# Attention scores of two mixers with high and low parts stacked to 128 rows

## The reference

```
# fox_branch, for each block of 128 queries
logits = (einsum('bhtd,bhsd->bhts', qb, kb) * scale + F[:, :, q0:q1, None] - F[:, :, None, :q1])
probs  = softmax(where(mask, logits, -inf));  outs.append(einsum('bhts,bhsd->bhtd', probs, vb))
# mixer_b, for each grid row
s = einsum('bnqhd,brnjhd->bhnqrj', q_r, k_reg) * scale + bias     # neighbourhood keys
s_ctx = einsum('bnqhd,bchd->bhnqc', q_r, kc) * scale              # context keys
p = softmax(concatenate([s, s_ctx]));  o = p_lat @ v_reg + p_ctx @ vc
```

## Time and profile before

| what | us |
|---|---|
| median of 3 runs | 3241.89 (3241.35 to 3244.12) |
| span of the profiled execution | 3236.3 |
| PE busy | 3109.7, 96% |
| DVE busy | 1999.7, 62% |
| ACT busy | 1299.9, 40% |
| POOL busy | 759.8, 23% |
| a turn of `fox` (first score to first score) | 77.0 |
| a turn of `nb` | 95.5 |

### The profile page before, as it was taken

How to read it: one execution, slowest core, us unless ns; L and a number is a source line. 1 busy time by engine, 2 the same in 40 slices (tenths; PEclk the granted TensorE clock), 3 DMA queues, 4 the chain that set the end, 5 groups by cost and what they waited for, 6 DMA issues and landing times.

```text
span 3236.3 us, 47842 instructions
## 1 busy us (share of the span) xinstructions
PE 3109.7 (96%) x18134; PEld 2578.9 (80%) x18134; DVE 1999.7 (62%) x3834; ACT 1299.9 (40%) x2340; POOL 759.8 (23%) x324
## 2 busy tenths in 40 slices
PE   9999999999999989999899999999899999999987
PEld 6888888777777767877799889888677778777765
DVE  5676677555565657975755555556755555655555
ACT  5534443444444440022444444440344444454412
POOL 3223332322222213543211121113112112111221
PEclk9999999999999999999999999999999999999999
DMA  3111111111111137521200010153201111100141
GB/s 118 46 40 46 46 59 46 60 59 53 53 53 53 64 146 298 220 79 52 91 30 30 31 43 30 46 203 130 78 21 51 45 51 45 51 32 33 67 161 76
DMA packets 64828, 237.79 MB, mean 73 GB/s; under 512 B 7008, under 2 KB 10080, under 8 KB 63600
## 3 DMA queue, kind: packets, MB, share of 16 engines
q1 hardware_dynamic: 31680, 115.91, 9.9%
q10 hardware_dynamic: 32944, 119.10, 9.7%
HBM read 185.11 MB, written 49.87 MB: 73 GB/s over the span
## 4 chain that ended last, share of the span: by engine, by line
PE 79%; DVE 9%; ACT 5%; issue 2%; DVEq 2%; DMA 1%; ACTq 1%; SPq 0%
PE ps L1304 21%; PE ps L189 13%; PE ps L360 9%; PE ps L2223 7%; PE ps L1368 5%; PE ps L1334 4%; PE ps L1350 4%; PE ps L891 3%; PE ps L482 3%; PE ps L868 2%; PE ps L133 2%; DVE fox_l L1455 1%; PE ps L852 1%; DVE wa_l L941 1%; PE ps L853 1%
## 5 line engine op out<-in xcount | busy, mean ns | idle before, releaser
L210 POOL TENSOR_TENSOR w_hi<-raw,small 128x1024 fp32r<-128x1024 f32 x160 | 334.9, 2093 | 2393.7 <-PE ps L1304 1099.3
L212 POOL TENSOR_TENSOR w_lo<-raw,w_hi 128x1024 fp32r<-128x1024 f32 x160 | 424.8, 2655 | 22.8
L1304 PE MATMUL ps<-nb_u_hi,w_hi 128*128 128x512 f32 (+1 forms) x640 | 249.2, 389 | 6.1 <-DVE nb_q_lo L2470 4.2
L1304 PE MATMUL ps<-nb_u_hi,w_lo 128*128 128x512 f32 (+1 forms) x640 | 246.6, 385 | 0.0
L1304 PE MATMUL ps<-nb_u_lo,w_hi 128*128 128x512 f32 (+1 forms) x640 | 245.7, 384 | 0.0
L1466 DVE TENSOR_TENSOR nb_pt_lo<-ps,nb_pt_hi 128x512 fp32r<-128x512 f32 x208 | 143.9, 692 | 144.2 <-ACT nb_pt_hi L1393 143.9
L360 PE MATMUL ps<-u_hi,w_hi 128*128 128x512 f32 x528 | 212.8, 403 | 5.9 <-ACT silu_h L539 2.6
L1304 PE MATMUL ps<-u_hi,w_lo 128*128 128x512 f32 x512 | 208.9, 408 | 0.0
L360 PE MATMUL ps<-u_hi,w_lo 128*128 128x512 f32 x528 | 208.6, 395 | 0.0
L360 PE MATMUL ps<-u_lo,w_hi 128*128 128x512 f32 x528 | 208.4, 395 | 0.0
L1304 PE MATMUL ps<-u_hi,w_hi 128*128 128x512 f32 x512 | 208.3, 407 | 0.0
(11 more groups left out here) (357 smaller groups left out, 8027.8 us busy)
## 6 DMA issues: line engine op xcount, KB each, us to landing
raw<-in_w_stream SPq DMA_DIRECT2D x160, 512.0 KB, 3.3
h_sb<-in_w_ada ACTq DMA_DIRECT2D x16, 1024.0 KB, 5.0
nf_b<-nf_rows ACTq DMA_DIRECT2D x16, 512.0 KB, 4.4
nb_bias<-in_rel_bias ACTq DMA_DIRECT2D x16, 448.0 KB, 3.8
y_parts<-wa_y_hi ACTq DMA_DIRECT2D x8, 640.0 KB, 3.0
y_parts<-wa_y_lo ACTq DMA_DIRECT2D x8, 640.0 KB, 4.2
la_out_yh<-y_parts SPq DMA_DIRECT2D x8, 640.0 KB, 10.0
la_out_yl<-y_parts SPq DMA_DIRECT2D x8, 640.0 KB, 11.1
```

Of the source, the lines that this page charges most:

```text
L210: pool.tensor_tensor(w_hi[:, s, :], raw[:, s, :], zero, ALU.add)
L212: pool.tensor_tensor(w_lo[:, s, :], raw[:, s, :], w_hi[:, s, :].bitcast(F32), ALU.subtract).then_inc(w_ready, 1)
L1304: mm = pe.matmul(ps[:, b:b + ch["n"]], w(slot, k), u[:, k, ch["c0"]:ch["c0"] + ch["n"]], start=k == 0 and p == 0, stop=k == KT - 1 and p == 2)
```

## The change

For each head there is now a set of operands of its own, with all 128 rows used:

- `q_hi[hd]`: the head's 64 channels of q_hi twice (rows 0 to 63 and 64 to 127); `q_lo[hd]`: q_lo on the head's own rows, zeros on the others.
- `k2[hd]`: k_hi on the head's own rows, k_lo on the others.

One pass q_hi[hd] x k2[hd] gives hi*hi + hi*lo, a second one q_lo[hd] x k2[hd] gives lo*hi. A piece is 4 matmuls of 128 rows (2 passes x 2 heads) instead of 6 of 64 rows. For this ACT writes a Q chunk in four copies of 64 rows and a K chunk in two, DVE each in two; the zeros are set once, by two memsets on DVE. To make room, `silu` shares the tile of `vt`, the window mask is a tile and a load of its own (its DMA stands behind that of `rope`), and `rows` has a place of its own. The wait of a score for `shifted` stands behind its other waits. The plan of steps is the same.

```diff
-                self.q_hi = sb(f"{n}_q_hi", [P, q_cols], F32R, area)
-                self.q_lo = sb(f"{n}_q_lo", [P, q_cols], F32R, area)
-                self.k_hi = [sb(f"{n}_k_hi{i}", [P, keys], F32R, area) for i in range(kv)]
-                self.k_lo = [sb(f"{n}_k_lo{i}", [P, keys], F32R, area) for i in range(kv)]
+                self.q_hi = [sb(f"{n}_q_hi{hd}", [P, q_cols], F32R, area) for hd in range(2)]
+                self.q_lo = [sb(f"{n}_q_lo{hd}", [P, q_cols], F32R, area) for hd in range(2)]
+                self.k2 = [sb(f"{n}_k2_{hd}", [P, keys], F32R, area) for hd in range(2)]
...
-                self.silu = sb(f"{n}_silu", [P, self.q_cols], at=area)
+                self.silu = self.vt[:, self.whole]
...
-                        for o0, key, n in runs:
-                            for p, (q, k) in enumerate(((self.q_hi, self.k_hi[kv]), (self.q_lo, self.k_hi[kv]),
-                                                        (self.q_hi, self.k_lo[kv]))):
+                        pe.wait_ge(self.shifted, s["n"] - 1)
+                        for o0, key, n in s["blk"]["pieces"][s["piece"]]["runs"]:
+                            for p, q in enumerate((self.q_hi, self.q_lo)):
                                 for hd in range(2):
-                                    r = rows_of(hd)
                                     o = (self.s_bank + hd) * CH + o0
-                                    mm = pe.matmul(ps[:, o:o + n], q[r, qc], k[r, key:key + n],
-                                                   start=p == 0, stop=p == 2)
+                                    mm = pe.matmul(ps[:, o:o + n], q[hd][:, qc], self.k2[hd][:, key:key + n],
+                                                   start=p == 0, stop=p == 1)
...
+            def queries_high(self, act, ch):
+                src, cols = self.projected(ch), slice(ch["c0"], ch["c0"] + ch["n"])
+                act.wait_ge(self.scored, ch["scored"])
+                for hd in range(2):
+                    for half in range(2):
+                        ins = nc.scalar.activation(self.q_hi[hd][rows_of(half), cols], src[rows_of(hd)], ACT.Copy,
+                                                   scale=HD ** -0.5)
+                ins.then_inc(self.high_out, 1)
...
+            def keys_high(self, act, ch):
+                src, cols = self.projected(ch), slice(ch["c0"], ch["c0"] + ch["n"])
+                act.wait_ge(self.scored, ch["scored"])
+                for hd in range(2):
+                    ins = nc.scalar.copy(self.k2[hd][rows_of(hd), cols], src[rows_of(hd)])
+                ins.then_inc(self.high_out, 1)
...
+            def keys_low(self, dve, ch):
+                src, cols = self.projected(ch), slice(ch["c0"], ch["c0"] + ch["n"])
+                dve.wait_ge(self.high_out, ch["out"][1])
+                for hd in range(2):
+                    r = rows_of(hd)
+                    ins = dve.tensor_tensor(self.k2[hd][rows_of(1 - hd), cols], src[r],
+                                            self.k2[hd][r, cols].bitcast(F32), ALU.subtract)
+                ins.then_inc(self.dve_out, 1)
+
+            def clear_halves(self, dve):
+                for hd in range(2):
+                    dve.memset(self.q_lo[hd][rows_of(1 - hd), :].bitcast(F32), 0.0)
...
+            nb.clear_halves(dve)
             nb.dve(dve, nb.lead, None, masks, evacuate, nb_tables)
```

73 lines of the change are left out of this document (34 added, 39 removed).

## The result

The changed kernel takes 3329.24 us (median of 4 runs, 3326.63 to 3332.15), the kernel before, run beside it, 3241.62. The ratio is 1.0271, with a 95% interval of 1.0257 to 1.0286. The direction was forecast, the size was not: 3292.7 with a range up to 3316, a step of 51 us, where 88 were measured.

The account below looks back on a forecast made before the run. PE, busy 96% of the span, was taken as the bound, so its waits cost full size. Costs of 75.6 us less 24.8 gained gave +50.8: span 3287.1, time 3292.7 us with 5.6 added, range 3252 to 3316.

Parts of the forecast that it names:

- PE's gain: Scores on PE: four 128-row matmuls for six save switching, at most 44.4 us; 24.8 kept after longer DVE hand-overs.
- Price of an evacuation: ACT and DVE: halving rows saves nothing, no overlap; a Q chunk of 512 costs ACT 1.83 us more, DVE 0.70.
- rival (a): Operations of 64 rows overlap after all, so each place is cheaper: costs 46.9 us, net +22, 3264; chance 0.13.
- Held Q chunk: Mid-turn, extra copies and low parts delay PE: 11.9 us over seven `fox` turns, 13.3 over seven of `nb`.
- Zeros and evacuations before the first `nb` turn: Before the first `nb` turn, two DVE memsets and second low parts lengthen PE's wait: 2.9 us.
- Turn's end of `fox`: `nf_tri` loses to POOL by 0.13; first score 3.2 us later, 3.5 booked, 24.5 over seven turns.
- Turn's end of `nb`: `nb_mid`'s first half beats POOL by 0.1, its second waits; first score 3.1 us later, 21.7 over seven turns.
- Rival (c): The near tie at the turn's end of `nb` is lost to POOL: 16.8 us more, 3309.5; chance 0.14.
- The sum: Whole kernel: 75.6 us of costs less 24.8 gained, +50.8; span 3287.1, time 3292.7; chance 0.38.
- rival (e): PE sets the pieces' pace, each gains in full (44.4 us), late chunks are caught up: -16, 3226; chance 0.10.
- (b): Only the near tie at the turn's end of `fox` is won against POOL: 16 us less, 3276.6; chance 0.12.
- (d): Operations of 64 rows overlap and PE keeps its whole 44.4 us: +2.5, 3244, no difference; chance 0.09.

Follow-up runs that it names:

- passes_alone: The kernel before with its own evacuations, but each piece's scores in four 128-row matmuls instead of six of 64 rows: 3225.6 us, ratio 0.994.
- evac_alone: The changed kernel's evacuations and tiles, but scores in three passes of 64 rows per head as before: 3352.04 us, ratio 1.0339.
- before_late_k: The kernel before with the last K chunk's low part made several times over, lengthening the wait before a turn's first score: 3313.46 us, ratio 1.022.

## Why the forecast was right in direction and wrong in size

- **PE's gain: mechanism right, both of its terms too large, and the net right in part by luck.** That the six matmuls cost like three, so that only the switching is saved, held. But some 28 us of work are gone where the forecast had 44.4: a piece of 512 keys gains 0.15 in the rows above and 0.11 to 0.13 on average in `passes_alone` (forecast 0.17), one of 128+256 keys 0.05 (forecast 0.16). Against that I had booked 44.4 - 24.8 = 19.6 for longer hand-overs; the idle time that goes with the passes is 8.5 in place (215.2 - 206.7) and 17.0 alone. The two errors have opposite signs, which is why the 24.8 come near the measured 22.8 (in place) and 17.6 (alone). Where DVE sets the pace, the interval of two pieces of `nb` grew from 2.81 to 2.98 (medians; forecast 2.93), and 20 pieces of `nb` wait instead of 11.
- **Price of an evacuation: right.** 2.39 for four copies (forecast 2.44), 1.39 for two low parts (1.40), no overlap; rival (a) fell.
- **Held Q chunk: right.** `fox` waits 2.48 where it waited 0.56, 1.9 more (1.7 forecast; with the old passes, in `evac_alone`, 1.6 more), `nb` 1.65 more (1.9).
- **Zeros and evacuations before the first `nb` turn: right.** PE waits 7.51 there instead of 4.17, 3.3 more (2.9 forecast).
- **Turn's end of `fox`: right**, near tie included: `nf_tri` lost by 0.15 (0.13 forecast), the first score waits 3.3 (3.2 forecast, with 3.5 booked).
- **Turn's end of `nb`: the near tie was called the wrong way.** I had `nb_mid` win by 0.1; it lost by 0.09 in four of seven turns. Won, the wait is 2.5 (3.1 forecast), lost 4.6 (5.5 forecast): 4 x 4.6 + 3 x 2.5 = 26 instead of 21.7. Rival (c) was right in half of the turns, and both of its prices were too high, so it matters little in the sum.
- **The step that failed: the working took every wait at its own length.** Under "The sum", 75.6 us of waits stand as 75.6 us of time. The waits were sized well: in `evac_alone` PE's idle time grew by 80.1. But behind most waits at a turn's start (all seven of `fox`, five of `nb`), and in `fox` behind five of the seven at the held chunk, PE runs at 1.2 GHz for 3.4 us. In all, 72 us more were spent at half speed, 61 of them in the turns, and that cost 33 us. `before_late_k` shows the price with nothing else changed.
- **The sum again, on spans.** The forecast was 3287.1, the changed kernel's span 3330.4, 43 more: +33 for the clock, which had no term; +17 for work that was not saved (28 instead of 44.4); -7 for waits (88.6, where 75.6 + 19.6 = 95.2 were booked). The signs of being wrong fit this: a turn of `fox` was to take 81.0 and takes 82.2 to 84.9, one of `nb` was to take 98.6 and takes 99.0 where the tie was won and the clock held, and up to 102.8 where not.
- **A hint was there.** The clock of 1.00 in the turns of before was read as a fact about the turns, and not as one about turns without long waits: the stretch with waits between the mixers has 41 us at half speed in the table above, and in `fox` the 7 us all lie in the last turn, behind a wait of 0.9 us.
- The faster rival (e) fell: the hand-over does set the pace at some pieces, and the held chunks were not absorbed. Rivals (b) and (d) fell too.

## What to carry to other kernels

A packing that saves matmuls has to be fed: count the instructions that write the packed operands, at full price for each half, and lay them on the chain that PE waits for. Price a new wait of 3 to 4 us on a PE that is otherwise busy at one and a half times its length, until a trace shows otherwise (here the mean of fourteen). Where two engines ask for the same thing within 0.2 us of each other, a forecast should carry both outcomes at about even chances, and the kernel should rather be changed so that the tie doesn't arise; here a finer signal and a table made later gave back 71 of the 88 us.
